# Hybrid decoder trunk, expert stages: a new turning of the inner activations and single 2 MB weight transfers

## The reference, cut to what matters

```
hid = jax.nn.silu(xblk @ w_gate[e]) * (xblk @ w_up[e])     # (tokens, 512)
return hid @ w_down[e]                                     # (tokens, 1024)
```

## Time and profile before

| | us |
|---|---|
| median of 3 runs | 1721.79 |
| the runs | 1758.09, 1719.36, 1721.79 |
| the profiled execution | 1725.76 |
| its span, first to last instruction | 1723.9 |
| TensorE busy in the span | 1655.6 (96%) |
| weight loads of TensorE (beside its matmuls) | 1089.4 (63%) |
| VectorE busy | 746.2 (43%) |
| ScalarE busy | 327.9 (19%) |
| mean rate of the DMA engines | 276 GB/s |

### The profile page before, as it was taken

The page is one execution under the profiler, slowest core; times in us unless marked ns, Lnnn a source line. Parts: engine busy times, 40 slices in busy tenths (PEclk is TensorE's granted clock), DMA queues, the critical chain, the costliest instruction groups (busy, mean ns, idle before and its releaser), DMA issues.

```text
span 1723.9 us, 24248 instructions
## 1 busy us (share of the span) xinstructions
PE 1655.6 (96%) x10111; PEld 1089.4 (63%) x10111; DVE 746.2 (43%) x1285; ACT 327.9 (19%) x545; POOL 77.0 (4%) x76
## 2 busy tenths in 40 slices
PE   8999998999999999989999999999999999999996
PEld 6876686555555555547787787878655555555553
DVE  4899744333333333334453444444423332333334
ACT  4224621001001000023221222222010101010002
POOL 0030001000000000000000000000100000000000
PEclk9999999999999999999999999999999999999998
DMA  8212138999999999984222122127699999999994
GB/s 298 98 55 92 60 148 332 399 403 401 397 408 405 399 399 405 407 342 147 76 71 98 49 98 98 66 102 317 225 398 404 405 405 410 405 406 399 401 403 198
DMA packets 109553, 475.29 MB, mean 276 GB/s; under 512 B 10752, under 2 KB 23040, under 8 KB 76544
## 3 DMA queue, kind: packets, MB, share of 16 engines
q1 hardware_dynamic: 101120, 455.11, 67.3%
q0 software_dynamic: 5248, 8.40, 1.7%
q10 hardware_dynamic: 3072, 10.18, 1.5%
HBM read 476.27 MB, written 6.29 MB: 280 GB/s over the span
## 4 chain that ended last, share of the span: by engine, by line
PE 85%; DVE 9%; DMA 2%; ACT 2%; issue 1%; SPq 0%; DVEq 0%; ACTq 0%; POOLq 0%
PE psum L921 25%; PE psum L945 13%; PE psum L836 9%; PE psum L837 9%; PE psum L838 9%; PE psum L1032 8%; DVE h L2056 2%; PE psum L912 2%; PE psum L1314 2%; DVE xs L1720 2%; PE psum L930 2%; DMA in_pair<-in_expert_w_up 1%; DVE w_lo L660 1%; PE psum L936 1%; PE psum L1204 1%
## 5 line engine op out<-in xcount | busy, mean ns | idle before, releaser
L2056 DVE TENSOR_TENSOR h<-h,psum 128x512 f32<-128x512 f32 x240 | 154.2, 684 | 248.1 <-PE psum L1032 248.1
L660 DVE TENSOR_TENSOR w_lo<-raw,w_hi 128x2048 fp32r<-128x2048 f32 x46 | 105.4, 2291 | 202.1 <-ACT w_hi L654 202.1
L945 PE MATMUL psum<-raw,hidT 128*64 128x512 f32 x672 | 155.0, 603 | 1.1 <-ACT hidT L1515 1.1
L654 ACT ACTIVATE w_hi<-raw 128x2048 fp32r<-128x2048 f32 x46 | 88.0, 1914 | 335.0 <-PE psum L838 334.9
L836 PE MATMUL psum<-w_hi,uT_hi 128*128 128x512 f32 x352 | 139.7, 397 | 3.6 <-DVE h L2174 1.4
L1533 ACT ACTIVATE y_hi<-psum,rt 128x512 fp32r<-128x512 f32 x62 | 42.6, 688 | 515.9 <-PE psum L1032 368.8
L838 PE MATMUL psum<-w_lo,uT_hi 128*128 128x512 f32 x352 | 137.8, 392 | 0.0
L837 PE MATMUL psum<-w_hi,uT_lo 128*128 128x512 f32 x352 | 137.8, 391 | 0.0
L1032 PE MATMUL psum<-y_hi,to_token 64*128 64x512 f32 (+1 forms) x464 | 107.7, 446 | 20.6 <-DVE h L2056 17.7
L2292 POOL DMA_INDIRECT x_e<-xs_dram,index x64 | 60.5, 946 | 1469.8 <-PE psum L912 787.9
L2035 DVE SCALAR_TENSOR_TENSOR y_lo<-psum,rt,y_hi 128x512 fp32r<-128x512 f32 x66 | 49.2, 748 | 137.5 <-ACT y_hi L1533 137.3
(11 more groups left out here) (252 smaller groups left out, 2509.8 us busy)
## 6 DMA issues: line engine op xcount, KB each, us to landing
raw<-in_expert_w_down SPq DMA_DIRECT2D x84, 1024.0 KB, 23.8
raw<-in_expert_w_up SPq DMA_DIRECT2D x44, 1024.0 KB, 23.6
free_a<-in_expert_w_gate SPq DMA_DIRECT2D x44, 1024.0 KB, 23.5
in_pair<-in_expert_w_up SPq DMA_DIRECT2D x42, 1024.0 KB, 23.7
in_uT<-in_expert_w_up SPq DMA_DIRECT2D x42, 1024.0 KB, 24.2
free_b<-in_expert_w_gate SPq DMA_DIRECT2D x40, 1024.0 KB, 23.4
in_pair<-in_expert_w_down SPq DMA_DIRECT2D x40, 1024.0 KB, 23.8
xs<-in_expert_w_gate SPq DMA_DIRECT2D x40, 1024.0 KB, 23.6
```

What stands on the lines that cost most here:

```text
L654: nc.scalar.activation(part(w_hi[half]), half_of(n, half, by_columns), ACT.Copy).then_inc(hi_ok[half], 1)
L660: nc.vector.tensor_tensor(part(w_lo[half]), half_of(n, half, by_columns), part(w_hi[half]).bitcast(F32), ALU.subtract).then_inc(lo_ok[half ...
L945: mm = nc.tensor.matmul(psum[c * FIRST:(c + 1) * FIRST, bank], x[:, j % 2, (j // 2) * FIRST:(j // 2 + 1) * FIRST], w[:, j, c * 512:(c + 1) ...
L2056: ins = V.tensor_tensor(dst, dst, psum[:, SUM_BANKS[half]], ALU.add)
```

## The change

It has two parts. First, w_down is laid out with four rows a partition: partition p holds rows 4p to 4p+3, 16 KB in one run, and chunk j of the down product is the rows 4p + j. So hid has to be turned with a step of four columns. In the narrow form this is done by 8 plain float32 matmuls with an identity as the moving operand instead of 2 transposes: for j = 0 to 3 and c = 0, 1 the 64 tokens on the partitions of half c, columns j, j+4, ... of the 256, against the 64x64 block of ident, into PSUM bank 4, the same partitions, 64 columns from 64j on. Each of them uses 64 rows and 64 columns of the array: c = 0 one corner, c = 1 the opposite one. The result has the same size; the down product's index into it changes. The wide form makes four transposes with a stepped operand. Second, the blocks 9 to 91 of each layer come as one transfer of 2 MB each, and only ready(0) waits for them; the first nine and the last four stay in halves (SPLIT).

```diff
+SPLIT = [n < RING or n >= len(BLOCKS) - 4 for n in range(len(BLOCKS))]
...
-        wd_dram = expert_w_down.rearrange("l e (j p) n -> l e p j n", j=HC)
+        wd_dram = expert_w_down.rearrange("l e (p j) n -> l e p (j n)", j=HC)
...
-        def ring_at(layer, n):
-
-            return 16 * (layer * len(range(n % RING, 3 * STEPS, RING)) + n // RING + 1)
+        def ring_at(layer, n, half):
+
+            counted = [k for k in range(n % RING, len(BLOCKS), RING) if SPLIT[k] or not half]
+            return 16 * (layer * len(counted) + counted.index(n) + 1)
...
                     w = ring[layer][n % RING]
+                    if not SPLIT[n]:
+                        sp.dma_start(w, one(source[kind], layer, at)).then_inc(ring_landed[n % RING][0], 16)
+                        continue
                     for half in range(2):
-                        if kind == "down":
-                            c = slice(half * HC // 2, (half + 1) * HC // 2)
-                            dst, part_of = chunks_of(w, HC)[:, c], one(source[kind], layer, at)[:, c]
-                        else:
-                            c = slice(half * HALF, (half + 1) * HALF)
-                            dst, part_of = w[:, c], one(source[kind], layer, at)[:, c]
-                        sp.dma_start(dst, part_of).then_inc(ring_landed[n % RING][half], 16)
+                        c = slice(half * HALF, (half + 1) * HALF)
+                        sp.dma_start(w[:, c], one(source[kind], layer, at)[:, c]).then_inc(ring_landed[n % RING][half], 16)
...
             def transpose_hidden(m, wide):
 
-                for j in range(HC if wide else HC // 2):
-                    mm = nc.tensor.transpose(psum[:, 4, j * P:(j + 1) * P], hid[:, j * P:(j + 1) * P], ident)
+                for j in range(HC):
+                    if wide:
+                        mm = nc.tensor.transpose(psum[:, 4, j * P:(j + 1) * P], hid[:, j:HID:HC], ident)
+                    else:
+                        for c in range(2):
+                            r = slice(c * FIRST, (c + 1) * FIRST)
+                            mm = nc.tensor.matmul(psum[r, 4, j * FIRST:(j + 1) * FIRST], hid[r, j:HID // 2:HC], ident[r, r],
+                                                  start=True, stop=True)
                 mm.then_inc(m.hidT_psum, 1)
...
-                                              x[:, j % 2, (j // 2) * FIRST:(j // 2 + 1) * FIRST],
+                                              x[:, j // 2, (j % 2) * FIRST:(j % 2 + 1) * FIRST],
...
                     def ready(half):
-                        pe.wait_ge(ring_landed[n % RING][half], ring_at(layer, n))
+                        if SPLIT[n] or not half:
+                            pe.wait_ge(ring_landed[n % RING][half], ring_at(layer, n, half))
```

More of the change, by code:

```diff
@@ L606, in one @@
             taken = src[layer, bass.ds(e, 1)]
-            return taken.rearrange("a p n -> p (a n)" if len(taken.shape) == 3 else "a p j n -> p (a j) n")
+            return taken.rearrange("a p n -> p (a n)")
         def copied(eng, *name):
@@ L789, in experts @@
                             for k, src in enumerate((wg_dram, wu_dram, wd_dram)):
-                                dst = over_w[k] if k < 2 else chunks_of(over_w[k], HC)
-                                sp.dma_start(dst, one(src, layer, e)).then_inc(over_landed[layer], 16)
+                                sp.dma_start(over_w[k], one(src, layer, e)).then_inc(over_landed[layer], 16)
                     sp.wait_ge(moe_done, layer + 1)
```

## The result

| | before | after |
|---|---|---|
| median, us | 1720.57 | 1768.52 |
| runs, us | 1718.77 to 1758.09 | 1765.34 to 1771.12 |
| span of the profiled execution, us | 1723.9 | 1768.3 |

The changed kernel is slower: a ratio of 1.028, 95% interval 1.0268 to 1.0293, so 48 us more. The forecast was 1742 us: the time lies in the range, but the loss is 48 us where 20 were expected. The medians are of all runs, while the ratios leave out single runs far above the others of their kernel (such as 1758.09 us here, 5109.61 in r3 and 4227.81 in r8).

The account below looks back on a forecast made before the run. TensorE was taken to bound the expert stage, transfers close behind. Turning +21.6 us and the vanished stall -1.4 us gave +20.2 us, so 1742 us; range 1735 to 1750, with some 8 in 10 from 1722 to 1772.

Parts of the forecast that it names:

- What bounds the stage: Expert stage: TensorE sets the end at 14.55 us a step, transfers close behind; a longer TensorE step is paid in full.
- The number of records and their pairs: Narrow turning: 16 loads and 16 matmuls instead of 2 and 2, in 8 slots with two corners side by side.
- I take it that corners, which share neither rows nor columns, do too: Narrow turning: the two opposite 64x64 corners run side by side, as column halves and row halves do, giving 8 slots.
- the slot of 0.06 us: Narrow turning: 8 slots of 0.06 us make 0.73 us instead of 0.37, 0.36 more a step, +21.6 us over 60 steps.
- the stepped operand: Narrow turning: reading the stationary operand with a step of four elements was counted as costing nothing.
- Rival C: Narrow turning: stepped float32 loads cost 0.11 us a slot of a pair, 0.71 us more, +41, 1763 us; chance 0.08.
- Rival B: Narrow turning: corners run one after the other, 16 slots of 0.06 us, 0.84 us more, +49, 1771 us; chance 0.18.
- The first nine blocks are as before, so the start of a stage doesn't change: Start of each layer's expert stage: no change in time expected from the new layout and transfers.
- The stall and the single transfers: End of layer 0's stage: wait for the last up block (0.5 us) and slower matmuls (0.9) go, -1.4 us; single transfers 0.
- E: Weight transfers: long runs lower the rate by 5%, 12 us a layer beside the forecast, 1766 us; chance 0.05.

Follow-up runs that it names:

- r3: Changed kernel, with VectorE writing hid sorted by chunk so that each corner's stationary operand is contiguous; 1737.54 us, ratio 1.0102 to the kernel before.
- r8: r3 with the two down blocks among a layer's first nine sent in quarters, runs of 4 KB; runs too unequal for a ratio, a repeat gave 1735.64 us.
- r5: Changed kernel without the second corner's matmuls, so half of the inner activations are not turned; one run, 1774.17 us.
- r4: Changed kernel, with the second corner of each pair writing bank 3 instead of bank 4, except in a layer's last step; one run, 1769.43 us.
- r1: Kernel before with only the single 2 MB transfers for blocks 9 to 91, old down layout and old turning; 1721.67 us, ratio 1.0005.

## Why the prediction was right or wrong

**What bounds the stage** was right. A longer TensorE step was paid in full: 60 x 0.73 = 43.8 us from the turning, 31 us back in r3 for 60 x 0.49 = 29.4. The transfers got their slack, the wait for the up block went.

**The number of records and their pairs** were right: 16 loads and 16 matmul records, in eight pairs that run side by side. "I take it that corners, which share neither rows nor columns, do too" held (r5). So did the slot of 0.06 us, for contiguous operands: r3's turning takes 0.61 us, where the sum had 0.73, and r3's 1737.5 us lie near the 1742 of the forecast. That is in part luck: the turning costs 60 x 0.24 = 14.4 us there, not 21.6, and 3 us are the later gather, which the forecast didn't have.

**The step that failed** is the stepped operand: "plain float32 loads of contiguous columns are slow already [...] so I count nothing for it". I had the row that spoke against it (0.202 against 0.140) and argued it away, since the plain load of contiguous columns looked as slow as the stepped transpose. But that plain load was of 128 columns (a slot of 0.12 us, L1235); 64 contiguous ones take half of it, 0.058 us in r3, so the row spoke of the number of columns and not of the step. The runs showed that the step adds its own price on top: 213 ns instead of 135, a slot of 0.12 us instead of 0.06, 0.49 us a step, 29 us in all. Rival C had it as a mechanism, with slots of 0.11 us and 1.08 us for the turning (1.10 measured), at a chance of 0.08. Its 1763 us were 5 short of the time, since it had the rest of the forecast, without the later gather.

**Rival B** had the time (1771) and the wrong cause. Its turning of 1.21 us is close to 1.10, and on the time alone it would have been confirmed. One corner left out (r5), the other bank (r4) and contiguous loads in the same bank (r3) speak against it: the turning is as long without the second corner, and in one bank as in two, and the pairs start together. The rule of the Trainium skill behind it ("TensorEngine Tiling (Array Packing)", "Gotcha 1: PSUM Pressure": different row tiles cannot access one bank at once) does not show in this case: two row halves that write different partitions of bank 4 start together, 0.058 us from pair to pair (r3). Two row halves that write the same partitions of a bank weren't tried.

**"The first nine blocks are as before, so the start of a stage doesn't change"** was wrong. They are still in halves, but the two down blocks among them have the new layout with runs of 8 KB. A store of rows that runs beside them took 3.3 us longer, and the first gather came 3.1 us later. I had looked at the order and the number of the transfers and not at their run length.

**The stall and the single transfers**: the wait went as said. In the traces the 1.4 us hold: the 0.5 us wait is gone and the last down product of layer 0 takes 3.61 us (4.53 before). In the times no run could show them (r1: 1.0005). E, a lower rate by longer runs, didn't happen: the ten slices of the page from 302 us (309 us after) on have a mean of 402 GB/s before and 403 after.

The sum with what the traces show: 43.8 + 3.1 - 1.4 = 45.5 us of 48. The remaining 2.5 us are within the scatter of the runs, and that scatter goes with the granted clock: the kernel before has 1718.80 us at a mean of 0.993 and 1721.54 at 0.989 (beside r1), the changed one 1765.34 and 1771.12. So the two are 46.5 us apart at 0.993 and 49.6 at 0.989. The spans of the two profiled executions are 44.4 us apart, the one before at 0.986 and the one after at 0.990. What is left beyond the sum at an equal clock, 1 to 4 us, stays open.

## What to carry to other kernels

When a layout moves a stride from a DMA into TensorE's stationary operand, price the load with the stride: here 16 bytes between float32 elements took a float32 load of 64 columns from 135 to 213 ns, 8 bytes nothing. In a stage where TensorE is the bound, half a microsecond in each of 60 steps is 30 us, while single transfers gave nothing that the runs could show. Two mechanisms with the same total (16 slots of 0.06, 8 slots of 0.12) are told apart by the start times and durations of single records, and by leaving one half out, not by the time.

## What the runs showed of the hardware that I had not expected

- A plain float32 load of 64 columns pays for a step of four elements (213 ns) but not for a step of two (135 ns); a float32 transpose's load of 128 columns pays for a step of two too (203 against 140 ns). Other steps weren't tried for plain loads, nor 128 columns, and why the line lies there stays open.
- Four stepped corner matmuls cost the same with or without four more in the opposite corner (1.10 us), in one bank or in two.
- A moving operand in pairs of elements 16 bytes apart streams 4.7% slower (3.77 against 3.60 us for 16 matmuls).
- Longer runs on one queue slow a transfer on another: the store of 2 MB beside two down blocks took 19.9 us with runs of 8 KB in them and 16.7 with 4 KB (r3, r8).
